# Two decoder layers on one core: four program blocks joined into one, with the weight fold moved into the attention stage

## What is computed

```
for i in range(2):
    shift, scale, gate = split(silu(c) @ ada_w[i] + ada_b[i], 3)
    h = rms_norm(x, norm_g[i]) * (1.0 + scale) + shift
    if i == 0:
        q, k, v, g = split(h @ w_in)            # 1024, 256, 256, 1024 columns
        q, k = rope(rms_norm(q)), rope(rms_norm(k))
        branch = (banded_sink_attention(q, k, v, sinks) * silu(g)) @ w_out
    else:
        v, g = split(h @ w_in)                  # 1024, 1024 columns
        mixed = (multiscale_pool(v) @ w_group) * pool_scale
        branch = (mixed * silu(g)) @ w_out
    x = x + gate * branch
```

## Time and profile before

| what | value |
|---|---|
| median of three runs | 1616.1 us (1610.34 to 1616.82) |
| the profiled execution | 1611.41 us, span 1609.7 us |
| PE busy | 1442.6 us, 90% of the span |
| DVE, ACT, POOL busy | 885.6, 542.0, 397.8 us |
| mean granted PE clock | 0.963 |
| DMA | 294.01 MB, mean 183 GB/s |

### The profile page before, as it was taken

One profiled execution on the slowest core, in us unless ns is written; L12 is line 12 of the kernel. 1 busy time (PEld: TensorE's weight loads), 2 busy tenths in 40 slices (PEclk: granted clock), 3 DMA queues, 4 the chain that ended last, 5 costly groups with the idle time before them and its releaser, 6 DMA issues. The chain is left out here.

```text
span 1609.7 us, 20167 instructions
## 1 busy us (share of the span) xinstructions
PE 1442.6 (90%) x7240; PEld 1216.9 (76%) x7240; DVE 885.6 (55%) x1513; ACT 542.0 (34%) x1262; POOL 397.8 (25%) x559
## 2 busy tenths in 40 slices
PE   2789999994799995689999999839999999999999
PEld 2577777783688884678888888638888788888787
DVE  7666666663434441787777774153446453455521
ACT  2433333432312221676656562131222222222210
POOL 2433333322033221575555553200000000000000
PEclk9999999997899997899999999969999999999999
DMA  7645555445877856755767765541112353111142
GB/s 283 234 160 193 198 196 197 175 170 233 333 291 277 336 206 225 282 188 217 273 232 281 270 255 178 200 132 53 52 41 85 112 193 111 49 53 50 58 147 86
DMA packets 96131, 294.01 MB, mean 183 GB/s; under 512 B 10752, under 2 KB 35360, under 8 KB 86304
## 3 DMA queue, kind: packets, MB, share of 16 engines
q1 hardware_dynamic: 87744, 262.28, 45.4%
q0 software_dynamic: 8288, 30.44, 5.2%
HBM read 200.41 MB, written 92.27 MB: 182 GB/s over the span
## 5 line engine op out<-in xcount | busy, mean ns | idle before, releaser
L1694 PE MATMUL po_f_ps<-po_ht,po_w 128*128 128x512 f32 x1536 | 352.1, 392 | 26.8 <-DVE po_ht L1597 26.8
L1694 PEld LDWEIGHTS po_f_ps<-po_ht,po_w 128*128 128x128 f32 x1536 | 290.3, 189 | 88.2 <-issue 17.2
L604 PE MATMUL qk_proj<-qk_w_qkv,qk_ht 128*128 128x512 f32 x1152 | 281.2, 400 | 14.9 <-DVE qk_w_qkv L489 7.8
L604 PEld LDWEIGHTS qk_proj<-qk_w_qkv,qk_ht 128*128 128x128 f32 x1152 | 216.2, 192 | 61.6 <-issue 9.7
L922 PE MATMUL ga_g_ps<-ga_ht,ga_w_g 128*128 128x512 f32 x768 | 182.9, 398 | 20.8 <-DMA ga_ht<-ht_split 20.8
L1332 PE MATMUL at_y_ps<-at_zt,at_w 128*128 128x512 f32 x768 | 196.1, 397 | 0.0
L922 PEld LDWEIGHTS ga_g_ps<-ga_ht,ga_w_g 128*128 128x128 f32 x768 | 146.1, 192 | 51.4 <-DMA ga_ht<-ht_split 21.2
L1708 PE MATMUL po_y_ps<-po_zt,po_w 128*128 128x512 f32 x768 | 176.9, 392 | 5.2 <-DVE po_zt L1622 5.2
L1708 PEld LDWEIGHTS po_y_ps<-po_zt,po_w 128*128 128x128 f32 x768 | 145.1, 189 | 36.3 <-DVE po_zt L1622 6.0
L1332 PEld LDWEIGHTS at_y_ps<-at_zt,at_w 128*128 128x128 f32 x768 | 137.7, 189 | 24.3
L1566 DVE TENSOR_TENSOR po_w<-po_raw,po_w 128x1024 fp32r<-128x1024 f32 x48 | 58.8, 1226 | 129.6 <-ACT po_w L1501 129.6
(11 more groups left out here) (152 smaller groups left out, 1735.9 us busy)
## 6 DMA issues: line engine op xcount, KB each, us to landing
at_w<-out_weight_split SPq DMA_DIRECT2D x32, 1024.0 KB, 6.1
ht_split<-qk_ht SPq DMA_DIRECT2D x8, 2048.0 KB, 9.4
queries_t<-qk_late SPq DMA_DIRECT2D x16, 1024.0 KB, 3.9
ga_ht<-ht_split SPq DMA_DIRECT2D x4, 4096.0 KB, 18.6
ga_ada<-in_ada_w POOLq DMA_DIRECT2D x64, 256.0 KB, 6.4
at_qt<-queries_t SPq DMA_DIRECT2D x16, 1024.0 KB, 7.6
values_split<-qk_late SPq DMA_DIRECT2D x16, 768.0 KB, 4.8
at_vs<-values_split SPq DMA_DIRECT2D x16, 768.0 KB, 4.8
```

The lines of the kernel that those rows point to most:

```text
L604: last = nc.tensor.matmul(proj[:, b * BANK:(b + 1) * BANK], ht[:, s % 2, m, k, t * P:(t + 1) * P], w_qkv[:, w, k, b * BANK:(b + 1) * BANK] ...
L1694: last = nc.tensor.matmul(f_ps[:, bank(j, h), :], w[:, i % 2, a, k, :], ht[:, h, m, k, :], start=(n == 0), stop=(n == 3 * KC - 1))
```

## The change

All four stages are written into one block, over one address map laid out so that the last part of a stage and the first of the next don't overlap. Each stage hands its predecessor functions that are called inside the predecessor's last part:

```diff
+        with nc.Block() as block:
+            @block.sync
+            def _(sp):
+                qk["sync"](sp, ga["first_load"])
+                ga["sync"](sp, at["first_load"])
+                at["sync"](sp, po["first_load"])
+                po["sync"](sp)
...
+            @block.tensor
+            def _(pe):
+                qk["tensor"](pe)
+                ga["tensor"](pe, qk["last_round"])
+                at["tensor"](pe, po["spread_first"])
+                po["tensor"](pe, at["last_sum"])
```

```diff
+    def first_load(sp, part):
+        if part == 0:
+            for i in range(RAW):
+                load(sp, i)
+        elif part == 2:
+            load(sp, RAW)
+            load_h(sp, 1)
+            load(sp, RAW + 1)
...
+        for stored in qk["stored"]:
+            pool.wait_ge(stored, 16 * NB)
...
+        for n in range(4):
+            load_ada(n)
```

```diff
+        def fold_high(u):
+            f = u // PAIRS
+            if u % PAIRS == 0:
+                act.wait_ge(wg_loaded[f % 2], 16 * (f // 2 + 1))
+                wait(act, fold_done, PAIRS * (f - 1))
+                nc.scalar.activation(wg[:, f % 2, HI], wg_raw[:, f % 2], ACT.Copy).then_inc(wg_hi, 1)
+            act.wait_ge(fold_loaded[u % 3], 16 * (u // 3 + 1))
+            wait(act, fold_done, u - 2)
+            nc.scalar.activation(wv[:, u % 3, HI], wv_raw[:, u % 3], ACT.Copy).then_inc(fold_hi, 1)
+
+        def fold_evict(u):
+            act.wait_ge(fold_done, u + 1)
+            wait(act, fold_stored[u % 2], 16 * GC * (u // 2))
+            nc.scalar.activation(folded[:, u % 2].rearrange("p c k n -> p k c n"), fold_ps[:, u % 2], ACT.Copy).then_inc(fold_out, 1)
...
+        def fold_low(u):
+            f = u // PAIRS
+            if u % PAIRS == 0:
+                dve.wait_ge(wg_hi, f + 1)
+                nc.vector.tensor_tensor(wg[:, f % 2, LO], wg_raw[:, f % 2], wg[:, f % 2, HI].bitcast(F32), ALU.subtract).then_inc(wg_lo, 1)
+            dve.wait_ge(fold_hi, u + 1)
+            nc.vector.tensor_tensor(wv[:, u % 3, LO], wv_raw[:, u % 3], wv[:, u % 3, HI].bitcast(F32),
+                                    ALU.subtract).then_inc(fold_lo, 1)
```

```diff
+    def load_n(pool, b, h, k):
+        u = norm_unit(b, h, k)
+        c = (HALVES * b + h) * KC + k
+        pool.wait_ge(at["x1_stored"][c % 3], 16 * (c // 3 + 1))
+        wait(pool, h_lo, u - 2)
+        pool.dma_start(x_n[:, u % 3, :], x1t_d[HALVES * b + h][:, k, :]).then_inc(n_loaded[u % 3], 16)
...
+            if i < FOLDS:
+                fold_low(i)
+        for c in range(CHUNKS - KC, CHUNKS):
+            next_lo(dve, c - CHUNKS + KC)
+            residual(c)
+            if c == CHUNKS - KC + 1:
...
+    def first_lo(dve, j):
+        norms(dve, 0, [(u // KC, u % KC) for u in (2 * j, 2 * j + 1)])
+        if j in (2, 4):
+            lo_w(dve, j // 2 - 1)
```

More of the change, by code:

```diff
@@ L182, in squared, with sync @@
         return 0, ()
-    def sync(sp):
+    def sync(sp, next_load):
         def load_x(s):
@@ L1372, in pool_layer, with pool_stage @@
+def pool_stage(nc, sem_of, dims, weights, ga, at, w_value, w_gate, w_out, scale_d, x1t_d, rstd1, mod1, ident, out_d):
+    KC, NB, GROUPS = (dims[n] for n in ("KC", "NB", "GROUPS"))
     TB = BANK
```

1938 lines of the change are left out of this document (1001 added, 937 removed).

## The result

The changed kernel takes 1560.65 us (median of four runs, 1558.77 to 1569.5), the kernel before 1616.46 (1610.34 to 1618.6). The ratio is 0.9671, with a 95% interval of 0.965 to 0.9692. The forecast was 1530 with a range up to 1559: the direction was right, the size was not, and the range missed by 1.7.

The account below looks back on a forecast made before the run. PE, busy 90% of the span, was held by waits mostly at stage starts (88 us in four lines). Terms summed to -85.3: 1526 from the profiled 1611.4, 1530.8 from 1616.1; forecast 1530, range 1509 to 1559.

Parts of the forecast that it names:

- The first gate chunk: Boundary one: the gate starts right behind the first transposes, at 376.4 instead of 406.7, -30.3 us.
- The gate stage: First gate chunk to last gate matmul: 184.9 us of work instead of 216.3, -31.4, with +3.5 coming back for late loads.
- I take 410.5: Gate stage: the time the ada loads land, taken from an estimate of 403 to 411.
- so it hides: Gate stage: the 4 MB load of h takes 10.4 us, is needed only in the second eight chunks, and costs nothing.
- The term of +3.5: Gate stage: a 2.4 us stall at chunk 6 for split weights, plus 1.1 for evictions and a weight load; ends 0 and 18.
- Rival (a): Boundary one: ada loads are late, first landing 10.4 us later and the next ring 5, total 1546; chance 0.17.
- Boundary two: Gate stage to attention: q, k and v loads issued in the last gate chunks remove the wait before the first scores, -18.8 us.
- The fold: Sixteen attention slots carry one fold each, lengthening the ACT and DVE chain to 5.7 us a slot, +27.0 (+10 to +37).
- Boundary three: Output chunks to pool stage: norm units move into the last 8 output chunks, -35.8 us, with +1.5 for their loads.
- the term for the norm loads: Last eight output chunks: a ring of three loads makes each of seven chunks 0.2 us too long, +1.5.
- My upper end of 10: Last eight output chunks: the norm loads' highest cost, for a landing of 8.5 us, 1.6 too long each.
- the prediction's own signs of being wrong: Fold slots under 5 or over 6.5 us, PE waiting over 6 in the first eight gate chunks, norm-unit output chunks over 6.

Follow-up runs that it names:

- g2: The changed kernel with ada additions starting in chunk 4 instead of 2, first modulation sum behind chunk 6 instead of 4: 1559.0 us, 0.9647.
- g1: The changed kernel with the 4 MB load of h issued later, behind the first weights of the output projection: 1565.0 us, 0.9679.
- g3: The changed kernel with the 4 MB load of h issued earlier, between the second-to-last tile's q and k stores: 1559.8 us, 0.9642.
- f1: The changed kernel with ACT's split and eviction of the fold between previous and p_hi instead of behind the exponentials: 1546.4 us, 0.9563.
- the last version: The changed kernel with ACT's fold moved, later sums, spread pool weights, x load behind weights, residual first, low part at once, h loads in four parts: 1526.2 us, 0.9449.

## Why the prediction was wrong, step by step

- **The first gate chunk**: right, -29.2 for -30.3. Stage one took 1.1 longer, which is less than its scatter: its end lies between 376.0 and 380.3 in kernels with the same code for it.
- **The gate stage**: this is the step that failed. The landing was forecast well, "I take 410.5" against a first addition at 412.3, in part by luck: the last k store took 14.3 to land, where I had counted 6 and another 7.8 for the weight loads beside it, and the first ada row took 3.2 for my 6.4. The 4 MB load, of which I said "so it hides", stood ahead of that store; with it moved away the store took 5.5. What was wrong was what is due then. I took the split weights of chunk 6 as the first thing that would be late, with three additions ahead of it. But PE's own list has the first modulation sum behind chunk 4, due at 408.7, and it needs eight additions, of which the last ended at 423.4. The term of +3.5 measured +25.1: 18.1 of waits and 7 of lower clock behind them, a cost that I gave to no stall. Rival (a) named late ada loads at the right place, and priced them by landings of 16.8; the stop came although the first four rows landed in 3.2 to 6.5, because of the due date. The runs add that a later due date takes the first stop from 14.88 to 3.52 (g2), and that the stops come back elsewhere when only one thing is changed (g1, g2, g3).
- **Boundary two**: right to 0.1.
- **The fold**: the mechanism was right and shown by the f1 run; the size was 30.7 for 27.0, from 16 units in 96.3. A slot took 5.90 where the sum of rows was 5.76 and I rounded down to 5.7; `fold_low` took 0.826 on average instead of 0.684 (more on that below), and the four slots with a group weight 6.50.
- **Boundary three**: the gap closed, and the pool stage's first pieces run without a pause. But the term for the norm loads, "+1.5", measured about 10: from the first output chunk to the end of the last one lie 324.4 instead of 312.4, and 1.7 of that are the spreads that now stand among them. I let three units share a round trip, 8.6 for three; the chunk's two scalings stand ahead of both low parts, so a buffer comes free late and two are under way: about 7.5 a chunk. With the low part at once DVE's waits for these loads fell from 18.0 to 5.6. I also left out that the residual stands behind these waits, and that SP's weight loads stand behind the landing of a store. My upper end of 10 was the right size by luck: it stood for a landing of 8.5 (and 7 times 1.6 is 11), while the median landing was 4.9. The estimate of 2.6 us for 256 KB, from the figure of the Trainium skill (DMA: Bandwidth & Descriptors, Anatomy of one DMA), would have made the term 0. Landings here were 3.0 to 8.8, so the measurement goes against using it in a stretch with other traffic.
- **The range**: its upper end held the ada case and a part of the norm loads, not both at their true size with the fold above its middle. The two terms for late transfers were low in the same way: each was priced at the lateness of one transfer, and neither at what stands behind the engine that waits for it. Two of the prediction's own signs of being wrong came true: PE waited over 6 in the first eight gate chunks (15.7), and output chunks with norm units took over 6 (7.2 each from 985.99 on).

What stays open: the shares of the DMA engines' load, of the four ada buffers and of DVE's list in the waits for sums, 17.2 in the changed kernel and 5.5 in the last version; and what of the fold's last 1.0 a slot is DVE's own time. Whether the norm loads would land sooner from SP's queue was not tried.

## What to carry to other kernels

When stages are joined, look on the waiting engine's own list for the first instruction that needs the late chain, and count all that must be done for it; the due date is there, not at the data that comes to mind. Work that is put into a latency-bound loop costs by the place of each instruction relative to the chain: with the same two instructions a slot took 5.9 or 5.0 us. When two in-order queues are late for the same engine, easing either alone moves the wait to the other. Look at what stands behind each wait for a landing, and at how many buffers are really in flight.

## What was not expected of the hardware

DVE's subtraction of two SBUF operands took 0.684 us in the gate stage, 0.826 on average in the attention slots and 1.10 in the slot shown above, where it began while POOL was masking. The one with an operand in PSUM did not get longer. The Trainium skill (SBUF — State Buffer, SBUF: two separate sides) says that a DVE instruction with two SBUF inputs and a POOL instruction that reads SBUF lock each other out for a whole instruction. By that, `fold_low` waits for the mask in progress, and the rows agree in both directions. Where a mask of POOL is in progress, `fold_low` ends 0.55 behind the mask's end, in the slots of the changed kernel (0.72 to 0.98) and of the run with ACT's part at another place (1.11). Where `fold_low` begins first, it keeps 0.68 and the mask gets longer: one that starts 0.01 behind it takes 1.16 instead of 0.63, and the pair 1.75 instead of 1.36.

```profile
607.52 1.75 POOL L1131 TENSOR_SCALAR_AFFINE_SELECT at_pt<-at_ph 128x512 fp32r<-128x512 f32 x2 [0.92 <-ACT at_ph L1182]
...
608.09 0.68 DVE L1297 TENSOR_TENSOR at_early_wv<-at_early_wv_raw,at_early_wv 128x512 fp32r<-128x512 f32 x1
```

No run took POOL's masks away.

The granted clock fell to 0.60 and 0.62 for some 4 us behind stops of PE of only 1.15 and 1.19 us in the gate stage, and stayed at 1.00 over 985 to 1000, in which PE stopped for 1.73 and 2.62. Behind 2.25 it was 0.83 over ten microseconds. The length of the last stop alone does not tell which. So a stop of a microsecond can cost more than another one: 96 matmuls behind one took 23.67, where the earlier trace rows have 22.07.
